# Router work of a hybrid decoder step done per chunk between the output projections, on unnormalised values

## The reference, cut to what matters

```python
mixed = sigmoid(gm_r) * (rnn @ w_br_rnn) + sigmoid(gm_a) * (attn @ w_br_attn)
x = x + mixed @ w_out
x = x + _hier_moe(_rmsnorm(x, ln2), w_rg, b_rg, w_re, b_re, w1, w3, w2)
x = x + sigmoid(_rmsnorm(x, ln3) @ w_ple_gate) * (p @ w_ple_proj)

def _hier_moe(h, ...):
    g_logit = h @ w_rg + b_rg                  # 4 groups, top 1
    g_prob, g_sel = softmax(g_logit), argmax(g_logit)
    e_logit = (h @ w_re + b_re).reshape(b, t, 4, 8)   # 8 experts in a group, top 2
    top_v, top_i = top_k(e_logit of the chosen group, 2)
    w_top = softmax(top_v) * max(g_prob)
    gates = sum(one_hot(g_sel * 8 + top_i, 32) * w_top)
    hid = silu(h @ w1) * (h @ w3)              # each expert: 2048 -> 256 -> 2048
    return sum over experts of (hid * gates) @ w2
```

## Time and profile before

| | |
|---|---|
| median of 3 runs | 1957.49 us (1956.63 to 1961.32) |
| profiled execution, its own time | 1956.76 us |
| span of the profile, first to last instruction | 1955.0 us |
| TensorE busy | 1816.6 us (93%) |
| VectorE busy | 1154.0 us (59%) |
| ScalarE busy | 880.4 us (45%) |
| mean granted TensorE clock | 0.955 of full speed |

### The profile page before, as it was taken

One profiled execution on the slowest core, in us unless ns is written; L12 is line 12 of the kernel. 1 busy time (PEld: TensorE's weight loads), 2 busy tenths in 40 slices (PEclk: granted clock), 3 DMA queues, 4 the chain that ended last, 5 costly groups with the idle time before them and its releaser, 6 DMA issues.

```text
span 1955.0 us, 23219 instructions
## 1 busy us (share of the span) xinstructions
PE 1816.6 (93%) x9628; PEld 1526.7 (78%) x9628; DVE 1154.0 (59%) x1373; ACT 880.4 (45%) x982; POOL 118.4 (6%) x75
## 2 busy tenths in 40 slices
PE   5999889747999999999999899999999999996998
PEld 3899768746877778997897777887887788884898
DVE  4985547897862222323442536886886788885533
ACT  3333355344443435321223235775665666663322
POOL 0100004231320010000000000000000000000000
PEclk9999889878999999999999579999999999999999
DMA  7443433322454354473555237997998899995540
GB/s 221 130 130 99 124 86 89 84 86 65 122 173 140 135 175 147 123 276 120 169 151 169 70 119 241 362 367 257 341 341 290 293 335 342 350 320 148 148 114 27
DMA packets 385912, 365.51 MB, mean 187 GB/s; under 512 B 18388, under 2 KB 361476, under 8 KB 383688
## 3 DMA queue, kind: packets, MB, share of 16 engines
q1 hardware_dynamic: 381704, 345.07, 56.7%
q0 software_dynamic: 4096, 18.88, 2.7%
HBM read 353.19 MB, written 10.72 MB: 186 GB/s over the span
## 4 chain that ended last, share of the span: by engine, by line
PE 83%; DVE 11%; ACT 3%; issue 2%; DMA 1%; POOL 0%; DVEq 0%; SPq 0%; ACTq 0%
PE psum L1577 22%; PE psum L770 18%; PE psum L783 9%; PE psum L1564 7%; PE psum L844 6%; PE psum L732 4%; PE psum L1742 2%; PE psum L1505 2%; PE psum L753 2%; PE psum L1764 1%; PE psum L616 1%; PE psum L1739 1%; PE psum L837 1%; DVE weights_low L2095 1%; DVE arena L2239 1%
## 5 line engine op out<-in xcount | busy, mean ns | idle before, releaser
L1001 DVE TENSOR_TENSOR weights_low<-arena,weights_high 128x2048 fp32r<-128x2048 f32 x192 | 439.7, 2292 | 103.1 <-ACT weights_high L870 102.9
L1577 PE MATMUL psum<-input_high,weights_high 128*128 128x320 f32 x1264 | 406.7, 322 | 47.9 <-ACT arena L1886 25.5
L870 ACT ACTIVATE weights_high<-arena 128x2048 fp32r<-128x2048 f32 x192 | 367.6, 1915 | 108.1 <-PE psum L783 58.3
L1577 PE MATMUL psum<-input_low,weights_high 128*128 128x320 f32 x1264 | 396.1, 313 | 0.0
L1577 PE MATMUL psum<-input_high,weights_low 128*128 128x320 f32 x1264 | 395.7, 313 | 0.0
L1577 PEld LDWEIGHTS psum<-input_high,weights_high 128*128 128x128 f32 x1264 | 243.0, 192 | 65.2 <-ACT arena L1886 30.7
L1577 PEld LDWEIGHTS psum<-input_low,weights_high 128*128 128x128 f32 x1264 | 243.5, 193 | 1.1
L1577 PEld LDWEIGHTS psum<-input_high,weights_low 128*128 128x128 f32 x1264 | 242.6, 192 | 0.1
L2095 DVE TENSOR_TENSOR weights_low<-arena,weights_high 128x1024 fp32r<-128x1024 f32 x128 | 150.9, 1221 | 112.3 <-ACT weights_high L1823 112.3
L770 PE MATMUL psum<-weights_high,gathered_high 128*128 128x512 f32 x512 | 213.6, 417 | 0.0
L1823 ACT ACTIVATE weights_high<-arena 128x1024 fp32r<-128x1024 f32 x162 | 162.0, 1051 | 93.6 <-PE psum L1577 64.2
(11 more groups left out here) (312 smaller groups left out, 2385.1 us busy)
## 6 DMA issues: line engine op xcount, KB each, us to landing
arena<-in_w SPq DMA_DIRECT2D x384, 512.0 KB, 5.6
arena<-in_w_in SPq DMA_DIRECT2D x64, 1024.0 KB, 5.6
arena<-in_w_out SPq DMA_DIRECT2D x16, 1024.0 KB, 5.9
arena<-in_w_ple_gate SPq DMA_DIRECT2D x16, 1024.0 KB, 6.2
arena<-in_w_br_rnn SPq DMA_DIRECT2D x8, 1024.0 KB, 5.3
arena<-in_w_br_attn SPq DMA_DIRECT2D x8, 1024.0 KB, 5.2
branch_spill<-arena SPq DMA_DIRECT2D x14, 320.0 KB, 6.6
arena<-branch_spill SPq DMA_DIRECT2D x1, 4480.0 KB, 16.7
```

The costliest lines, as they stand in the source:

```text
L870: nc.scalar.activation(stage[m % STG][0][:], mslots[m % MRING], ACT.Identity).then_inc(s["high"], 1)
L1001: v.tensor_tensor(lo[:], mslots[m % MRING], hi[:].bitcast(F32), ALU.subtract).then_inc(s["split"], 1)
L1577: last = mm(acc[0:m, 0:T], x[:, P * k:P * k + m], y[:], start=(k == 0 and n == 0), stop=(k == KD - 1 and n == 2))
```

## The change

The sums, logits and transposes of the second norm are made on `x * ln2` without the token's factor 1/root (`xg`, a ring of 8 chunks padded with zeros to 384 tokens), one chunk after each output projection:

- TensorE: `router_pe` after each unit `out` k. After unit 3 it transposes `ptok` and does chunks 0 to 2, after unit k > 3 chunk k-1, by `turn_chunk`: three logit matmuls and three transposes. Chunk 15 and one set of three sums over the channels follow the last unit.
- VectorE: `router_dve` makes `xg`, and adds the squares of the chunks to one tile `sq_sum` (before, TensorE summed 16 tiles). ScalarE: `router_act` squares, and copies the turned chunks to `htok`.
- SyncE: the outputs of the states, the router's weights and `ptok` move from behind all loads of `w_out` to ahead of the load for unit `out` 4 (`router_loads`). The first expert loads wait for the split of the last tile instead of the last unit.
- The token factor enters in two places: the logits are multiplied by `rstd3` (128x3 instead of a 128x320 root), and the selection `S` holds `rstd3` instead of 1, so that the fill gives normalised rows. `ST` is made 0/1 again by a comparison, and the gates are multiplied by the root.
- Order behind it: `select(0)` comes before the gates, `fill` before `places`, the flags for overfull groups move behind expert slot 20 (`overfull`), and VectorE's three register loads behind the last expert.

```diff
+        def turn_chunk(pe, k):
+            pe.wait_ge(xg_ready, k + 1)
+            for tt in range(3):
+                mm_last = nc.tensor.matmul(bank(2 + tt)[:, 0:36], xg[:, k % XG, P * tt:P * (tt + 1)], wr[:, k, :],
+                                           start=(k == 0), stop=(k == KD - 1))
...
+            if a == 0 and q:
+                pe.wait_ge(ht_cp, 3 * q)
+            for tt in range(3):
+                last = nc.tensor.transpose(bank(5 + tt)[:, P * a:P * (a + 1)], xg[:, k % XG, P * tt:P * (tt + 1)], ident)
+            last.then_inc(xg_used, 1)
...
         def second_pe(pe, sum_sq):
+            turn_chunk(pe, KD - 1)
+            pe.wait_ge(*freed(first_out + KD - 2))
+            pe.wait_ge(ss_mm, 2 * KD)
+            for tt in range(3):
+                last = mm(bank(even_out)[:, 4 * tt:4 * tt + 4], sq_sum[:, P * tt:P * (tt + 1)], C("ones")[:, 0:4],
+                          start=True, stop=True)
...
-            pe.wait_ge(router_done, 1)
-            pe.wait_ge(ht_cp, 12)
...
-            places(0)
             for q in range(4):
                 fill(0, q)
+            places(0)
...
+        def router_act(act, k):
+            if k == 1:
+                act.wait_ge(states_out, 64)
+                act.wait_ge(ss_mm, KD + 1)
+            if k:
+                router_square(act, k - 1)
+            if k >= 5 and k % 4 == 1:
+                for tt in range(3):
+                    turn_copy(act, k // 4 - 1, tt)
...
+        def router_dve(dve, k):
+            if k == 0:
+                nc.vector.memset(xg[:, :, T:TP], 0.0)
+                dve.wait_ge(states_out, 64)
+                nc.vector.memset(sq_sum[:, T:TP], 0.0).then_inc(ss_mm, 1)
...
+            nc.vector.tensor_scalar(xg[:, k % XG, 0:T], XT[:, k, :], vec[:, V_LN2 + k:V_LN2 + k + 1], None, ALU.mult
+                                    ).then_inc(xg_ready, 1)
+            if k:
+                router_add(dve, k - 1)
+            if k == 3:
+                dve.wait_ge(pre_t, 3)
+                nc.vector.tensor_copy(pT[:], psum[:, 5:7, 0:T]).then_inc(p_cp, 1)
...
+            link(v.tensor_tensor(lg[:], psum[:, 2:5, 0:36], wide(rstd3, 36), ALU.mult))
...
+                    last = v.tensor_scalar(S[:, tt, :], C("iota"), pos[:, tt, g:g + 1], rstd3[:, tt, :], ALU.is_equal,
+                                           ALU.mult)
...
+                if m == 20:
+                    overfull()
...
+            more = dve.value_load(flags_i[0:1, 0:1], min_val=0, max_val=2)
+            groups = [dve.value_load(flags_i[0:1, n:n + 1], min_val=0, max_val=NG - 1) for n in (1, 2)]
             with dve.If(more > 0):
...
-            sp.wait_ge(acc_ready, len(units))
+            sp.wait_ge(tile_split, 2 * NT)
...
+                if loads[n][1] == first_out + 4:
+                    router_loads(sp)
                 weight(n)
```

More of the change, by code:

```diff
@@ new lines, in router_pe @@
+        def router_pe(pe, k):
+            if k == 3:
+                pe.wait_ge(ple_in, 32)
+                for j in range(2):
+                    for tt, (t0, n) in enumerate(TILES):
+                        last = nc.tensor.transpose(bank(5 + j)[:, t0:t0 + n], ptok[0:n, tt, P * j:P * (j + 1)],
+                                                   ident[0:n, 0:n])
+                last.then_inc(pre_t, 1)
+                pe.wait_ge(router_in, 64)
+                pe.wait_ge(p_cp, 1)
+                for i in range(3):
+                    turn_chunk(pe, i)
+            elif k > 3:
+                turn_chunk(pe, k - 1)
@@ L591, in second_pe @@
             pe.sem_inc(main["used"], STG)
[L592 to L623, removed]
@@ L629, in second_pe @@
             for t2 in range(3):
[L630 to L631 removed]
+                last = mm(bank(even_out)[:, 32:36], C("ones"), goh[:, t2, :], start=(t2 == 0), stop=(t2 == 2))
             last.then_inc(cum_mm, 1)
[L633 to L634 removed]
             def experts(s, g):
                 pe.wait_ge(s["select"], g + 1)
[L639 to L642, removed]
+                for tt in range(3):
+                    nc.tensor.transpose(bank(3)[:, P * tt:P * (tt + 1)], S[:, tt, :], ident)
@@ L643, in experts @@
+                for tt in range(3):
+                    last = mm(bank(3)[:, TP:TP + NE], S[:, tt, :], gates[:, tt, :], start=(tt == 0), stop=(tt == 2))
                 last.then_inc(s["st_mm"], 1)
@@ L1093, in second_dve, with wide, every @@
-            groups = [dve.value_load(flags_i[0:1, n:n + 1], min_val=0, max_val=NG - 1) for n in (1, 2)]
+            gmax, gexp, gsum, eqs, r_a, r_b = r1
+            em, gt, pe_, eq, cum = rt
+            def wide(ap, n):
+                return ap.broadcast_to((P, 3, n))
+            def every(ap, n):
+                return ap.rearrange("p (t k) -> p t k", t=1).broadcast_to((P, 3, n))
+            link(v.tensor_scalar(w4[:], C("iota")[:, 0:4], -1.0, 5.0, ALU.mult, ALU.add))
+            dve.wait_ge(x2_var_mm, 1)
@@ new lines, in second_dve @@
+            dve.wait_ge(goh_ready, 1)
+            link(v.tensor_scalar(r_b[:], goh[:], BIG, -BIG, ALU.mult, ALU.add))
+            link(v.tensor_tensor(em.rearrange("p t (g e) -> p t g e", g=NG),
+                                 lg[:, :, NG:36].rearrange("p t (g e) -> p t g e", g=NG),
+                                 r_b.rearrange("p t (g e) -> p t g e", e=1).broadcast_to((P, 3, NG, EPG)), ALU.add))
+            for t in range(3):
+                last = v.max(v8[:, t, :], em[:, t, :])
+            link(last)
@@ new lines, in second_dve, with select @@
+            v.tensor_tensor(pe_[:], em[:], wide(v8[:, :, 0:1], NE), ALU.subtract).then_inc(rl_x, 1)
+            dve.wait_ge(cum_mm, 1)
+            link(v.tensor_tensor(pos[:], bank(even_out)[:, 16:28].rearrange("p (t g) -> p t g", t=3), goh[:], ALU.mult))
+            def select(g):
+                for tt in range(3):
+                    last = v.tensor_scalar(S[:, tt, :], C("iota"), pos[:, tt, g:g + 1], rstd3[:, tt, :], ALU.is_equal,
+                                           ALU.mult)
+                last.then_inc(main["select"], 1)
@@ new lines, in second_dve @@
+            select(0)
+            low(main, 0, 0)
+            link(v.tensor_tensor(gt[:], em[:], wide(v8[:, :, 1:2], NE), ALU.is_gt))
+            link(v.tensor_tensor(eq[:], em[:], wide(v8[:, :, 1:2], NE), ALU.is_equal))
+            link(v.tensor_reduce(r_a[:, :, 0:1], gt[:], AX_X, ALU.add))
+            link(v.tensor_scalar(r_a[:, :, 0:1], r_a[:, :, 0:1], -1.0, 2.0, ALU.mult, ALU.add))
+            for t in range(3):
+                last = v.tensor_tensor_scan(cum[:, t, :], eq[:, t, :], eq[:, t, :], 0.0, ALU.add, ALU.bypass)
```

296 lines of the change are left out of this document (143 added, 153 removed).

## The result

The changed kernel took 1897.55 us (median of 4 runs, 1892.07 to 1902.48) beside 1959.4 us for the kernel before on the same chip: a ratio of 0.9682, with a 95% interval of 0.9649 to 0.9715.

What follows compares the result with a forecast made beforehand. The 89.9 us stage between projections and experts, partly at half clock, was taken as the bound; 89.9 - 20.8 - 42.7 - 1.0 - 2.1 = 23.3 us less than 1956.76 gave 1933.5, range 1916 to 1942.

Steps and rivals of the forecast that it cites:

- What bounds the kernel: Between last projection and first expert: 89.9 us of chained steps, with TensorE's clock falling to 1.2 GHz.
- Chunks between the projections: Projection stage: 14 chunks of logit matmuls and transposes at 1.12 us each add 15.6 us, bounds 13.2 and 24.8.
- The dear price for 36 columns: Rival in the projections: a 36-column record costs 0.227 us, 9.2 us more, time 1942.7; chance 0.05.
- The two stalls: Projections: TensorE waits 2.8 us at unit 2 for VectorE's state-output wait, 2.4 us behind unit 3 for the `ptok` copy.
- The rival of lost projections: Projections fall to 1.2 GHz, 7.06 us more a unit; all 13 from unit 3 give +92, 2025; chance 0.03.
- Chain behind the last unit: From the last projection unit's end to the fill's start: 10.2 us, bounds 8.5 and 12.5.
- Fill and places: Ahead of the first expert: fill at 1.2 GHz as now, 30.0 us, then places, 2.5 us.
- the clock rival: The first fill gets its full clock: 16.1 us instead of 30, time 1917.4; chance 0.12.
- Given back later: Flags ahead of an expert split cost 1.0 us (bounds 0 and 2.8); register loads behind the last expert cost 2.1.
- the third line of the table: Stage from the first expert matmul to the end of the last: forecast +1.0 us.
- the second line: Stage from the end of unit 15 to the first expert matmul: forecast -47.2 us.

Runs made afterwards that it cites:

- the grouped form: Changed kernel with the third token tile at 64 rows, a quarter's four 64-row fill matmuls standing together behind its eight 128-row ones: 1899.77 us, one run.
- before with 128 rows: Kernel before, with only the fill changed to use 128 rows for the third token tile, unused rows zeroed once: 1920.26 us, ratio 0.9793.
- the run with 64 rows throughout: Changed kernel with all three token tiles of the fill at 64 rows, the other tokens left out of the gather: 1913.82 us, one run.
- the mixed fill with everything else changed: Changed kernel, but the fill's gather matmuls use 64 rows for the third token tile again (128, 128, 64 in turn): 1934.56 us, ratio 0.9873.
- the two runs with 64 rows throughout: Changed kernel with all fill tiles at 64 rows, and 16 and 4 unread 128x128 matmuls behind the last unit: 1899.53 us (1892.35 and 1906.7).
- the version with all three edits: Changed kernel plus earlier state outputs and `ptok`, unread matmuls behind the last unit, spread flags and earlier register loads: 1883.28 us, again 1883.09.
- the mixed fill behind a busy TensorE: Changed kernel with fill rows 128, 128, 64 in turn, and 16 and 4 unread 128x128 matmuls behind the last unit: 1921.04 us, two runs.

## Why the prediction was wrong

*What bounds the kernel* was read rightly: the 90 us between the last unit and the first expert, and a clock at half speed in it.

*Chunks between the projections*: right in kind, a little too dear. 6 logit records and 3 transposes take 0.59 + 0.36 = 0.95 us at the full clock, forecast 1.12; 14 are 13.3 us instead of 15.6. The dear price for 36 columns did not come.

*The two stalls*: right in place and nearly in size (about 2.2 us each, forecast 2.8 and 2.4). Not in the sum were the falls of the clock behind them, 3.1 us. That this line came out right, +21.1 us measured and +20.8 forecast, is luck: the falls cancel what the chunks and stalls were too dear. The rival of lost projections is refuted; each fall lasted some 3 to 4 us and made only the unit in which it came longer.

*Chain behind the last unit*: 1083.65 to 1095.24, 11.6 us instead of 10.2. The table load is on it as said; the counts ran at the low clock throughout (2.69 + 1.29 us for the 2.9 taken).

*Fill and places*: **the step that failed.** The sum took the fill "at 1.2 GHz as now: 30.0 us". It was 12.8, and the places 0.9 instead of 2.5. The reasoning on the clock ahead of it held, for the clock was at 0.50 when the fill began. The error was to carry over the price of a fill whose matmuls the change had altered. The 128 rows stood in the text only as a point for the clock rival. That rival came nearer, but its 16.1 us were four mixed quarters of 4.03, so it had the wrong price too: at the full clock this fill takes 10.98.

*Given back later*: the flags cost TensorE a wait of 1.3 us, forecast 1.0, and the register loads lengthen the tail (2.8 us in all, forecast 2.1). But the third line of the table has a gain of 18.2 where I had a loss, **and that term was missing altogether.** The same `fill` serves groups 1 to 3, and 12 quarters save 1.35 us each and 0.19 each in the expert matmuls behind them, 18.5; the first 72 expert matmuls no longer start at the half clock, 17.85 against 16.77, 1.1 more. The `places` of the later groups are padded to 128 rows too: their matmuls take 0.59 instead of 0.90 us, before and then after,

```profile
1208.93 0.90 PE psum L717 x6
```

```profile
1162.30 0.59 PE psum L735 x6
```

and with their transposes (0.33 instead of 0.42) three of them save 1.2. Against it stand the 1.3 and the fall of the clock at 1710 to 1714, which the second profile of the changed kernel does not have: that one's experts are 1.6 us shorter (605.8). Together the gain is 17.9 of the 18.2.

The fill and the missing term account for the whole miss: 17.2 + 1.6 - 1.4 = 17.4 in the second line and 19.2 in the third make 36.6; the other two lines came out 1.0 us dearer than forecast; that leaves 35.6, against the 35.5 by which the sums in the table differ. And the rest of the forecast can be tested by itself: the run with everything but the 128 rows of the fill took 1934.56 us, where 1933.5 had been forecast for the whole. As a gain on its own chip that is 26.6 us against 23.3; the closeness of the two times is in part luck.

No row of before prices a change of rows, but a bound was to be had: in the earlier trace rows 24 records of a fill take 4.03 us, 0.168 each, and 8 transposes of as many columns 1.09, 0.136 each. At that price 12 quarters of 3.27 us would have saved 9 us, and the range would have begun lower; I gave the edit no bound at all.

Of the sentence that I had weighed, the Trainium skill, "TensorE: Matmul & The Clock Gate", Part 1, that "activity releases the throttle": the traces of after, of the grouped form and of before with 128 rows agree with it, the run with 64 rows throughout does not, with TensorE busy for 20 of 20 us at 0.50. I was wrong to dismiss it for the changed kernel by a row of a fill with other rows.

## What to carry to other kernels

Price every line of a diff by the shape of the instructions it leaves, the lines that look like tidying too: a pad that only makes a tile whole was worth 37 of the 62 us here, because the loop that it stands in runs 16 times, because TensorE paid 0.19 us at each change between 64 and 128 rows, and because the clock came back inside the first fill. Where a narrow tile can't be padded, put its matmuls together (1899.77 us in one run, against 1934.56). And before a stretch at the low clock is taken over into a forecast, look at what TensorE did in it and whether the change alters that: here the clock came back inside every traced first fill that began at 0.50 with 128-row matmuls in sequence, and inside one of the four whose rows were mixed or 64 throughout.

## What the runs showed of the hardware that I had not expected

A change between 64-row and 128-row fp32 matmuls costs 0.19 us at the full clock, and (30.05 - 20.84)/31 = 0.30 at the low one, the fill having 31 of them. TensorE can be 100% busy for 28 us at 0.50: the mixed fill with everything else changed shows it as the earlier trace rows did.

```profile
1092.00:1120.00 28.00, 28.00 (x93) 21.31 (x91) 9.48 (x22) 2.39 (x4) 0.00 (x0) 0.50 0.35 113
```

The same idle time or thin work does not always make the clock fall: behind the wait for `ptok` it fell in one profile of the changed kernel and not in the other, behind the first stall it fell in both and stayed at 1.00 in the two runs with 64 rows throughout, and in the first of the two profiles of the version with all three edits it was at 0.50 from 1081 to 1084, its first fill taking 12.44 instead of the 10.98 of the second, with the same matmuls around it. With the mixed fill behind a busy TensorE it fell about 1.6 us ahead of the fill, with four unread 128-row matmuls in between, and came back 2 us into it. So keeping TensorE busy with unread matmuls kept the clock in three of the five traces that tried it. What decides this is left open; no run was aimed at it.
